# A residual stream kept with features on partitions through a four-block transformer kernel: down products with stationary weights, norms as sums over partitions, 1/rms applied after the products

## What is computed

```python
def rmsnorm(x, w): return x * rsqrt(mean(x * x, axis=-1) + 1e-6) * w
def swiglu(h, w_up, w_down):
    gate, up = split(h @ w_up, 2)
    return (silu(gate) * up) @ w_down
for i in range(2):                                   # the first block
    x = x + 0.5 * swiglu(rmsnorm(x, n1), wu1, wd1)
    h = rmsnorm(x, mix_norm[i])
    x = x + mixer_i(h)      # gated delta rule + retention, then dilated + differential attention
    x = x + 0.5 * swiglu(rmsnorm(x, n2), wu2, wd2)
x = rmsnorm(x, final_norm)
for l in range(2):                                   # the second block
    h = rmsnorm(x, norm_g[l]) @ w_in[l]
    kv = rmsnorm(mem, mem_norm_g[l]) @ w_mem_kv[l]
    y = concat(moba(h), hgrn(h), memory_attention(h, kv)) * silu(z)
    x = x + y @ w_out[l]
```

## Time and profile before

| | us |
|---|---|
| median of 3 executions | 1663.26 |
| the 3 executions | 1661.27, 1663.4, 1663.26 |
| span of the profiled execution (first to last instruction of the program) | 1660.5 |

### The profile page before, as it was taken

How to read it: one execution, slowest core, us unless ns; L and a number is a source line. 1 busy time by engine, 2 the same in 40 slices (tenths; PEclk the granted TensorE clock), 3 DMA queues, 4 the chain that set the end, 5 groups by cost and what they waited for, 6 DMA issues and landing times.

```text
span 1660.5 us, 26122 instructions
## 1 busy us (share of the span) xinstructions
PE 1561.8 (94%) x10738; PEld 1427.0 (86%) x10738; DVE 961.9 (58%) x1107; ACT 749.1 (45%) x923; POOL 57.7 (3%) x48
## 2 busy tenths in 40 slices
PE   6999999897999989999997899999999899899988
PEld 6999999886999989999886799998999568899856
DVE  4544567537554554545576645457676665478644
ACT  4333457315333353333535433337546564544643
POOL 0000000010000000000000000000021000013000
PEclk9999989999999999999999999999999789999969
DMA  7445524204555544555431654555443224424202
GB/s 296 178 178 193 186 102 152 77 26 157 203 177 186 190 165 178 179 182 195 166 129 52 235 181 178 181 196 176 151 172 127 76 93 153 173 103 152 102 1 77
DMA packets 35732, 252.17 MB, mean 152 GB/s; under 512 B 4000, under 2 KB 4256, under 8 KB 6080
## 3 DMA queue, kind: packets, MB, share of 16 engines
q1 hardware_dynamic: 33120, 238.84, 39.7%
q0 software_dynamic: 2528, 12.13, 2.1%
HBM read 249.90 MB, written 1.05 MB: 151 GB/s over the span
## 4 chain that ended last, share of the span: by engine, by line
PE 84%; DVE 8%; ACT 5%; issue 2%; DMA 1%; SPq 0%; DVEq 0%; ACTq 0%; POOL 0%
PE ps L832 25%; PE ps L833 24%; PE ps L834 24%; PE ps L947 4%; ACT w_hi L1191 1%; DVE act_lo L1505 1%; DVE w_lo L1448 1%; PE ps L1089 1%; PE ps L1062 1%; DVE xn L1500 1%; PE ps L1104 1%; ACT work L1364 1%; PE ps L1102 1%; PE ps L1078 1%; ACT pair L1229 1%
## 5 line engine op out<-in xcount | busy, mean ns | idle before, releaser
L1448 DVE TENSOR_TENSOR w_lo<-raw,w_hi 128x2048 fp32r<-128x2048 f32 x226 | 520.4, 2306 | 371.5 <-ACT w_hi L1191 370.2
L832 PE MATMUL ps<-act_hi,w_hi 128*128 128x256 f32 x2304 | 665.8, 289 | 26.7 <-DVE act_lo L1505 17.8
L833 PE MATMUL ps<-act_lo,w_hi 128*128 128x256 f32 x2304 | 657.0, 285 | 0.0
L834 PE MATMUL ps<-act_hi,w_lo 128*128 128x256 f32 x2304 | 656.8, 285 | 0.0
L1191 ACT ACTIVATE w_hi<-raw 128x2048 fp32r<-128x2048 f32 x226 | 431.2, 1910 | 342.1 <-PE ps L834 335.8
L832 PEld LDWEIGHTS ps<-act_hi,w_hi 128*128 128x128 f32 x2304 | 447.4, 194 | 34.9 <-issue 23.5
L833 PEld LDWEIGHTS ps<-act_lo,w_hi 128*128 128x128 f32 x2304 | 447.6, 194 | 4.6 <-issue 3.1
L834 PEld LDWEIGHTS ps<-act_hi,w_lo 128*128 128x128 f32 x2304 | 447.1, 194 | 0.0
L832 PE MATMUL ps<-w_hi,act_hi 128*128 128x256 f32 (+1 forms) x448 | 152.0, 339 | 4.5 <-issue 3.0
L834 PE MATMUL ps<-w_hi,act_lo 128*128 128x256 f32 (+1 forms) x448 | 145.8, 325 | 0.0
L833 PE MATMUL ps<-w_lo,act_hi 128*128 128x256 f32 (+1 forms) x448 | 145.6, 325 | 0.0
(11 more groups left out here) (224 smaller groups left out, 1363.0 us busy)
## 6 DMA issues: line engine op xcount, KB each, us to landing
raw<-panels SPq DMA_DIRECT2D x226, 1024.0 KB, 4.8
gain<-gains POOLq DMA_DIRECT2D x10, 512.0 KB, 4.0
xn<-mem_in POOLq DMA_DIRECT2D x2, 1024.0 KB, 5.2
table<-tab POOLq DMA_DIRECT2D x1, 1472.0 KB, 6.2
table<-tab POOLq DMA_DIRECT2D x1, 1216.0 KB, 8.1
x<-x_in SPq DMA_DIRECT2D x1, 1024.0 KB, 4.9
out<-x POOLq DMA_DIRECT2D x4, 256.0 KB, 2.3
table<-tab POOLq DMA_DIRECT2D x1, 832.5 KB, 6.5
```

The costliest lines, as they stand in the source:

```text
L832: pe.matmul(o, l[0], r[0], start=start, stop=False)
L833: pe.matmul(o, l[0], r[1], start=False, stop=False)
L834: return pe.matmul(o, l[1], r[0], start=False, stop=stop)
L1448: tt(w_lo[:, s], raw[:, s], w_hi[:, s].bitcast(F32), ALU.subtract).then_inc(panel_lo, 1)
```

## The change

`x` now has features on partitions throughout (8 blocks x 256 tokens). `down` keeps the weights stationary and streams the 256 tokens (48 products for a panel); the last stage `out2_1` alone keeps the old form, under the name `down_rows`, and adds to `x_rows`, to which `turn_back` and `rows_back` bring `x` during the last attention. The gain is a value for each partition and goes into the splitting of a block; the sum of squares over features is a sum over partitions (squares on ScalarE, three additions on GpSimd, two products with a matrix of ones on TensorE), and 1/rms, the same on all partitions (`r_b`), is multiplied into the products where they are evacuated: gate and silu in `ffn`, the first 12 panels of `in0` (which VectorE evacuates now), the rope tables of `in1`, and a column form `r_c` for panels in the form "rows". `pre0` and `pre1` multiply it in before the splitting (`norm_x`). The first panel of each stage runs block by block as the blocks are split (`up_by_column`). The gains come as one small load. The table of the first mixer is loaded at the start. The cut diff:

```diff
+EVACUATED_BY_DVE = {("in0", k) for k in range(12)}
 def norm_steps(tag):
+    for b in range(PAIRS):
+        out.append(("dve", "residual", (before, b)) if before else ("dve", "keep_x", (b,)))
+        out += columns(tag, b) + [("act", "sq", (tag, b))]       # columns: x_hi, x_lo of two blocks
+    out += square_sums(tag)                                      # pool add 1, 2, 3
+    return out + (late_splits_of(before) if before else [])
 def ffn_steps(f):
+    return norm_steps(tag) + [("pe", "gate_first", (f,)), ("pe", "norm_sum", (tag,)), ("pe", "ffn", (f,)), ("act", "rstd", (tag,)), ("act", "ffn", (f,)), ("dve", "ffn", (f,))]
...
 def order():
-    out = [("sp", "load", (x,)) for x in ("x", "gain_ffn0", "const", "small")]
+    out = [("sp", "load", (x,)) for x in ("const", "x", "gains")]
+    out += [("pool", "load", ("small",)), ("pool", "zero", ()), ("pool", "load", ("tab1",)), ("act", "logs", ())]
+    out += [("pe", "turn_gains", ()), ("dve", "gain_cols", ())] + [("pe", "turn_x", ("ffn0", b)) for b in range(PAIRS)]
...
+        out.append(product)
+        if p == 0:
+            out += [("pe", "norm_sum", ("mix0",)), ("act", "rstd", ("mix0",)), ("pe", "ab_mm", ())]
+        if p == 1:
+            out += [("pe", "rstd_rows", ("mix0",)), ("dve", "rstd_cols", ("mix0",))]
+        out += [evacuate, ("act", "tap", (p,)), ("dve", "conv", (p,))] + [("act", "conv_silu", (p - 1,))][:p] + late
...
+    out += [(e, k, a) for b in range(PAIRS) for e, k, a in (("dve", "residual", ("ffn3", b)), ("act", "sq", ("final", b)))]
+    out += square_sums("final") + late_splits_of("ffn3") + first
+    out += [("pe", "norm_sum", ("final",)), ("act", "rstd", ("final",))] + others[0]
+    out += [(e, k, a) for b in range(PAIRS) for e, k, a in
+            (("dve", "final_x", (2 * b,)), ("dve", "final_x", (2 * b + 1,)), ("act", "sq", ("pre0", b)))] + square_sums("pre0")
     for l in range(2):
+        if l:
+            out += [("pe", "norm_sum", ("pre1",)), ("act", "rstd", ("pre1",))] + others[0]
+        out += others[1]
+        if not l:
+            out += [("pe", "norm_sum", ("pre0",)), ("act", "rstd", ("pre0",))]
+        product, evacuate, *late = others[2]
+        out += [product] + scaled(f"pre{l}") + [evacuate] + late
...
+            out += panel_steps("out2_0", None, 0, 4) + turns + all_columns("mem1") + panel_steps("out2_0", None, 4)
...
+            def add(tag, b):                                     # GpSimd
+                pool.wait_ge(act_done, at("act", "sq", tag, b))
+                nc.gpsimd.tensor_tensor(pair[:, 0:512], pair[:, 0:512], pair[:, 512 * b:512 * b + 512], ALU.add).then_inc(pool_done, 1)
+            def up_by_column(slot, bank, form, n, tag):          # TensorE
+                for c in range(DC):
+                    pe.wait_ge(dve_done, at("dve", "x_lo", tag, c))
+                    for half in (0, 1):
+                        ins = product(slot, bank, form, half, c, c == 0 and half == 0, True, [slot_of(tag, i) for i in range(DC)])
             def down(slot, parts, first, last, n, j=None, step=0):
+                for d in range(DC):
+                    for c in range(2):
+                        o = ps[:, d // 2, SEQ * (d % 2):SEQ * (d % 2) + SEQ]
+                        ins = three(o, weight(slot, c, P * d, P, D), [a[:, c, :] for a in parts],
+                                    first and c == 0 and d % 2 == 0, last and c == 1, True)
+                    if last and d % 2 and d < DC - 1:
+                        ins.then_inc(bank_ready, 1)
                 def gate_up(i, j=None):
+                        pe.wait_ge(gate_scaled, of(j, c + i, 2))
+                        up(n % SLOTS, 4, "cols", n, j, 6, slots=slots)
                         pe.wait_ge(gate_read, of(j, c + i, 2))
+                    up((n + 1) % SLOTS, 5, "cols", n + 1, j, 6, slots=slots)
+            def norm_sum(tag):
+                pe.wait_ge(pool_done, at("pool", "add", tag, PAIRS - 1))
+                pe.matmul(ps[:, 7, 0:SEQ], cst("ones"), pair[:, 0:SEQ], start=True, stop=False)
+                pe.matmul(ps[:, 7, 0:SEQ], cst("ones"), pair[:, SEQ:2 * SEQ], start=False, stop=True).then_inc(pe_done, 1)
...
+            def x_hi(tag, c):                                    # ScalarE
+                nc.scalar.activation(act_hi[:, slot_of(tag, c)], src, ACT.Copy, scale=gain_col(tag, c)).then_inc(act_done, 1)
+            def x_lo(tag, c):                                    # VectorE
+                finish(stt(act_lo[:, s], src, gain_col(tag, c), act_hi[:, s].bitcast(F32), ALU.mult, ALU.subtract))
             def residual(name, b):
+                finish(stt(x[:, c], grid(ps[:, b], 2), k, x[:, c], ALU.mult, ALU.add))
+            def evacuate(name, k):                               # VectorE, in0 panels 0 to 11
+                finish(tt(to, grid(ps[:, bank_of(name, k)], 2), rb(2), ALU.mult))
+                # VectorE, ffn gate_up
+                    tt(grid(gate_x, 2), grid(ps[:, 4], 2), rb(2), ALU.mult).then_inc(gate_scaled, 1)
                     split_lo(n + 3, j, 6)
                     dve.wait_ge(silu_done, of(j, c + i + 1, 2))
+                    tt(grid(silu_buf, 2), grid(silu_buf, 2), rb(2), ALU.mult).then_inc(silu_scaled, 1)
```

435 lines of the change are left out of this document (279 added, 156 removed).

## The result

The changed kernel took 1670.85 us (median of 4 runs) beside 1663.33 us for the kernel before: ratio 1.0044, 95% interval 1.0026 to 1.0062. Six more runs of the same kernel in a later comparison gave 1673.23 us beside 1664.27, ratio 1.0062 (1.0041 to 1.0082). So it is slower by about 0.5%, some 8 us; the prediction said 1659.5 us, 4 us faster.

What follows compares the result with a forecast made beforehand. TensorE, busy for 94% of the span, was the bound; 16.2 - 20.5 - 4.2 - 1.3 + 0 + 6.6 - 5.0 + 3.4 + 1.0 = -3.8 us took the span to 1656.7, plus 2.8 for the median: 1659.5 us, range 1649 to 1670.

Steps and rivals of the forecast that it cites:

- Down panels, +16.2: 58 of 64 down panels with stationary weights go from 5.48 to 5.76 us, +0.28 us each, all on the path.
- Rival C: Chance 0.04: 48 down products of 256 columns take 5.48 us a panel, the 16.2 us vanish, and the kernel takes 1643.
- Boundaries: Norms: T ends the last down product; second panel at T + 7.4, not T + 12.0; ffn1/ffn3 -6.2 each, ffn2 -8.1.
- the first split behind the blocks ends at T + 7.4, when it is needed: At a norm, VectorE's first weight split is ready in time, 7.4 us after the last down product ends.
- mix1, -4.2: The norm before mix1 saves 4.6 us, less 0.4 for turning 1/rms into columns.
- Queues passed: At the norms, a check of work queued on VectorE: the first split is in time, 1.4 us more a gate round fits.
- Start, -1.3: Start and ffn0: the early table delays panel 1 from 26.1 to 26.4, but the 1.41 us wait goes: -1.3 us.
- in0, 0: In in0 VectorE becomes the bound with 6.9 us rounds, but TensorE's lead cancels the losses: 0, between -4 and +6.
- rival B: Chance 0.18: VectorE paces in0 and the delta chain, the stage is 7 to 8 us longer, and the kernel takes 1667.
- ffn3 to in2_0, +6.6: From ffn3 to in2_0's first panel: +6.6 us, with TensorE waiting 5.3 us before pre0's sum behind a late `final_x`.
- out2_0 to in2_1, -5.0: From out2_0's end to the end of in2_1's first panel: 33.0 us instead of 38.0, with memory blocks split earlier.
- Last attention, +3.4: In the last attention, 16 more transposes at half clock, 0.22 us each, without idle time: +3.4 us (0 to +4).

Runs made afterwards that it cites:

- e4: The changed kernel without GpSimd's 27 additions of squares, each sum taking only the last pair's squares: 1663.42 us, ratio 1.0009 to the kernel before.
- The first experiment: The changed kernel with VectorE's products for lambda moved ahead of mix1's norm steps and the weight splits: 1666.11 us, ratio 1.0023 to the kernel before.

## Why the prediction was wrong, point by point

The largest term was right. The steps that failed, the largest first, are the list of what stands in the queues behind the norm at mix1, the length of the first split at a boundary, the lead that was to cancel the losses in in0, and the start; on the other side, the price of the transposes in the last attention was too high.

*Down panels, +16.2.* Right: 0.30 us a panel measured, against 0.28. Undoing this alone gave 16.5 us. Rival C is refuted, and the issue gap that pointed to it doesn't hold for these products. The Trainium skill ("TensorE: Matmul & The Clock Gate", section "Back-to-back issue gap") gives that formula for an isolated product, which the prediction left out; its figure there for a stream with a weight load each, 131 ns at 512 columns, is still further from the 228 of this trace.

*Boundaries.* The mechanism was right: the second gate panel comes at T + 14.35 where it was 19.4 to 21.3, and the 1.41 us are gone. The term was 1.15 us too good at each. The step "the first split behind the blocks ends at T + 7.4, when it is needed" took 2.29 us for a split that runs beside an addition, where it takes 3.30. The trace of before had the sign, and I didn't look: at 1264.14 a split takes 3.11 us,

```profile
1264.14 3.11 DVE L1448 TENSOR_TENSOR w_lo<-raw,w_hi 128x2048 fp32r<-128x2048 f32 x1
```

beside an operation of GpSimd that began at 1262.68 and took 2.42. The Trainium skill ("SBUF — State Buffer", section "Who interferes with whom") has a rule for it: a VectorE instruction with two inputs in SBUF and a GpSimd instruction that reads SBUF exclude each other, the later one waiting for the earlier to end. By this rule the split of 417.78 would start at 418.93 and end at 421.22; it ended at 421.08, and e4's split took 2.29: the trace agrees, within 0.14 us. With it in the sum, the five boundaries would have been 5 us worse.

*mix1, -4.2.* Missed by 5.6 us, the largest single error. The step "Queues passed" named the splits of weights and not what stood behind them, `lam_mul`, for which TensorE waited 3.48 us. The first experiment shows 4.1 us of it.

*Start, -1.3.* x landed at 6.7 us (I took 9.2), panel 0 at 12.8 (13.7), the first product came at 15.3 (16), and the first panel ended at 24.6 (25.1). But panel 1 started at 27.45 (26.4), after a wait of 1.69 us for its split: ScalarE takes its half of that split only behind the last `x_hi` and square. ffn0's end was 3.0 us later instead of 1.8.

*in0, 0.* The round was right (6.77 against 6.9), the wait before the decay chain too (5.86 against 6). The chain's first product was to come 56.4 us behind T and came after 58.7, so the lead that I let cancel the half clock and the later evacuations wasn't there: +3.0, inside my bounds. This is rival B at half its strength.

*ffn3 to in2_0, +6.6.* 7.4 measured (6.5, and 0.9 of the 4.0 in ffn3, which hold eleven downs at 3.1): the wait at pre0 was seen and its cause named, 6.87 us against 5.3, because `final_x` takes 5.89 us beside GpSimd's additions and 4.13 without them.

*out2_0 to in2_1, -5.0.* Right in kind and size: -4.5.

*Last attention, +3.4.* In the two profiles compared the attention's stretch grew by only 0.2 us (39.9 to 40.0), and 1.1 came off a wait of TensorE for ScalarE in in2_1 (3.26 to 2.13). The step "in rounds in which TensorE has no idle time" priced 16 transposes at half clock, and took the length of the half clock as given. With the transposes the full clock came back 3 us sooner in this profile, and 10 us sooner in eleven of the fourteen; the stage is then 2.4 to 3.1 us shorter than without them (39.8). What brings it back stays open.

The sum was off by 10 us: 5.6 at mix1, 3.6 at three boundaries, 3.0 in in0 (mix0's boundary in it), 1.2 at the start and 1.7 in small parts, against 4.1 from the last attention and 1.0 of restarts that had been set apart. Against the -3.8 us that were forecast, the span of this profile grew by 5.6 us, and the median by 7.5. Rival B had the right sign, but its mechanism alone made only 3 us.

## What to carry to other kernels

When a stage is shortened, list everything that stands in the queues between its start and the next product, not just the large operations: 0.3 us of VectorE work behind two splits cost 4 us. Where an idle engine is given work, look in the trace of before for what happens to its neighbours while it runs; the price of GpSimd's additions was VectorE's splits. And a change in the layout that loses 0.5% can hold a gain that is only a matter of order: three reorderings and a later table took 1671 us to 1653, below the 1662 of the kernel before, with the 16 us of dearer down panels still in.

## What the runs showed of the hardware

- VectorE and GpSimd take turns when both read two operands from SBUF: a split of 2.29 us takes 3.30 beside an addition, two `x_lo` 1.84 instead of 1.00, and an addition of 1.30 that begins under a split takes 3.16 us. Without GpSimd's additions the splits behind a norm are back at 2.29. At final's norm in the changed kernel each waits for the other in turn: the addition ends 1.2 us after the first split, and the second split 2.2 us after the addition.

```profile
1139.68 2.86 DVE L1628 TENSOR_TENSOR w_lo<-raw,w_hi 128x2048 fp32r<-128x2048 f32 x1
...
1140.54 3.16 POOL L871 TENSOR_TENSOR pair<-pair 128x512 f32<-128x512 f32 x1
...
1142.47 3.38 DVE L1628 TENSOR_TENSOR w_lo<-raw,w_hi 128x2048 fp32r<-128x2048 f32 x1
```

- A stage with more work in it was mostly the shorter one: behind a wait of 4.83 us TensorE, busy without a gap in small products, ran at half clock until 28 to 30 us behind the start of the wait. With 16 transposes added the full clock returned 10 us sooner in eleven of fourteen profiles, and the stage took 37 us, not 40. In one of the fourteen it returned 4 us later than without them, and the stage took 42.5. What decides between them stays open.
- The same 68 matmuls took 12.8 or 17.0 us from profile to profile, with the granted clock (1.00 or 0.70). That is 4 us, as much as most single edits here give, and the changed kernel's ten runs spread from 1667.2 to 1677.8 us; the waits between engines named above repeat to 0.01 us. Single causes are better read from these than from totals.
